# Convolution taps regrouped around the waits of VectorE in a fused encoder layer

## The chip, the cores and the metric

One core of a Trainium2 chip (trn2) runs the whole kernel as one launch. The metric is the device time in microseconds (us), lower being better. Names of engines: PE is TensorE, DVE is VectorE, ACT is ScalarE, POOL is GpSimd, SP is SyncE.

## What is computed

One layer of an encoder for 16 meta tokens, a prompt of 512 frames and a sample of 32 frames with cached keys, values and convolution rows. All in float32, model width 1024, 16 heads of 64, convolution width 31. Cut to what matters:

```python
glu, q, k, v, gates = _in_proj(_rmsnorm(x, g_mix), w_in)      # glu = a * sigmoid(b)
y = depthwise_conv(ctx, w_dw) + b_dw                          # 31 taps, causal, per channel
conv_out = silu(_layernorm(y, g_ln, b_ln)) @ w_pw2
z = q . k * HEAD_DIM ** -0.5                                  # per head, strictly causal mask
log_1m = where(mask, log_sigmoid(-z), 0.0)
tail = cumsum(log_1m, reverse=True) - log_1m
attn_out = where(mask, exp(log_sigmoid(z) + tail), 0.0) @ v
x = x + (sigmoid(g_conv) * conv_out + sigmoid(g_attn) * attn_out) @ w_out
x = x + square(relu(_rmsnorm(x, g_mlp) @ w_up)) @ w_down
y_out = _rmsnorm(x, g_final)
```

Outputs are y for both groups, the new keys and values, and the last 30 GLU rows of each group.

## The kernel before

Activations lie transposed, channels on the 128 partitions and up to 560 tokens along the free axis. Each matrix product is done in three passes of split operands (high by high, high by low, low by high); a weight tile of 1024 x 128 is split by ACT (w_hi, and the negated raw copy in w_lo) and finished by a DMA that adds the raw tile to w_lo.

After loading and normalising x comes the channel loop: eight turns, i = 0 to 7, one for each block of 128 channels, which are two heads and 128 convolution channels. A turn has six projections on PE, each 48 matmuls: q (unit 0), k (unit 1), v (unit 2), a (unit 3), b (unit 4), gate of the attention (unit 5). Turn 0 is written out, and turns 1 to 7 are one hardware loop. Every engine runs its own list in order, as written by hand, and waits on counting semaphores. PE's list in turns 1 to 7 is: units 0 and 1; `cumulate` of the second head of the turn before; unit 2; `values` of the turn before (the product with v, into PSUM bank 3 and a part of bank 1); `scores` of the first head; the transposes of v; units 3 and 4; `cumulate` of the first head; unit 5; `scores` of the second head.

In `scores` of the first head, banks 0 and 2 are done first. Bank 1 still holds the sample's 32 columns that `values` has left there, so PE waits for `mix_s_done` before the masks that open that bank:

```python
                if not early:
                    pe.wait_ge(mix_s_done, i)
                    masks_1()
```

This is the mask L639 that stands behind the matmuls of 144 columns (L635) in the timeline. `mix_s_done` comes from the first instruction of DVE's `gate_mix` (L1372), which reads those columns; L1373 reads bank 3. `gate_mix(prev)` itself waits for `pv_done` (PE's `values`) and `ga_done` (ACT).

`softplus_logs` on ACT turns scores into log(1 + exp(-|z|)) (L1014, L1019, L1024), DVE's `softplus_sum` (L1401) adds max(z, 0), `tile_sums` (L1419 to L1434) folds sums over tiles, ACT rounds (L1032, L1036), and DVE forms the low parts (L1407 and, in `sums_low`, L1438). `cumulate` on PE (L671, L691) needs these, and needs L1438 for its products with `negones`; ACT then takes exponentials (L1048). For the convolution's gate, ACT computes its logarithm (L1002 to L1006) from unit 4, DVE subtracts (L1490), ACT takes the exponential (L1113), and DVE multiplies into `conv_in` (L1492). The attention's gate goes likewise over L1002 to L1006 and DVE's L1377.

The 31 taps of the depthwise convolution are DVE instructions over 574 columns (L1362 for taps 0 and 1, L1365 for the rest), one for each tap and block. Taps of channel block i start at the end of turn i (groups 0 and 1 of the list `CONV`), and the rest is spread over turn i + 1 between the steps that other engines wait for, by `conv_before(n)`, which does group n. Turn 0 has no block before it. The block of turn 7 is finished behind the loop, in one string of 20 taps. L1515 behind the loop is the last step like L1438; a load of weights into the ring's fourth slot on SP waits for it.

Of the kernel before, what the change touches and what calls it, by code (L numbers as in the profile page):

```python
# [24 lines left out]
TAPS = 31  # L25
# [59 lines left out]
def build(nc, x_prompt, x_sample, cache_k, cache_v, cache_conv, meta, g_mix, w_in, w_dw, b_dw,  # L85
# [25 lines left out]
    with ExitStack() as ctx:  # L111
# [180 lines left out]
        def tile(i, t):  # L292
            return X_TILES + LOOP_TILES * i + t
# [27 lines left out]
        def cols2(ap, half):  # L321
            return ap.rearrange("p (h c) -> p h c", c=half)
# [17 lines left out]
        def x_half(t, h):  # L340
            (_, col, n), = X_COLS[t]
            return xT[:, h * KC // 2:(h + 1) * KC // 2, col:col + n]
# [199 lines left out]
        def _(pe):  # L542
# [63 lines left out]
            def scores(i, hh, first=False):  # L606
# [47 lines left out]
                for j in (2, 3):  # L654
                    bank, off, _, q0 = KT[j]
                    mm = score_split(bank, off, j, q0)
                mm.then_inc(z_scored, 1)
# [3 lines that stand above are left out]
                bank, off, _, q0 = KT[1]  # L661
                score_split(bank, off, 1, q0)
                score_last().then_inc(z_scored, 1)
# [642 lines left out]
        def _(dve):  # L1306
# [50 lines left out]
            def conv(i, taps):  # L1357

                for k in taps:
                    src, w, dst = conv_in[:, META + k:META + k + CONV_COLS], cw_cur[:, PAD + k:PAD + k + 1], acc[:, k % 2, :]  # L1360
                    if k < 2:
                        nc.vector.tensor_scalar(dst, src, w, None, ALU.mult).then_inc(tap_done, 1)  # L1362
                    else:
                        dve.wait_ge(tap_done, TAPS * i + k - 1)
                        nc.vector.scalar_tensor_tensor(dst, src, w, dst, ALU.mult, ALU.add).then_inc(tap_done, 1)  # L1365

            def gate_mix(i):

                mixed_cur = mixed[:, bass.ds(i, 1), :].rearrange("p n c -> p (n c)")
                dve.wait_ge(ga_done, i + 1)  # L1370
                dve.wait_ge(pv_done, i + 1)
                nc.vector.tensor_tensor(mixed_cur[:, SEQ:], z[:, 1, S_PV:S_PV + DEC], gate_a[:, SEQ:], ALU.mult).then_inc(mix_s_done, 1)  # L1372
                nc.vector.tensor_tensor(mixed_cur[:, 0:SEQ], pv[:], gate_a[:, 0:SEQ], ALU.mult).then_inc(mix_done, 1)  # L1373

            def attn_gate(i):
                dve.wait_ge(ga_ln, i + 1)
                nc.vector.scalar_tensor_tensor(cols2(gate_a[:], HALFO), psum2(1, HALFO), 0.0, cols2(gate_a[:], HALFO), ALU.min, ALU.subtract).then_inc(ga_log, 1)  # L1377
# [8 lines left out]
                nc.vector.tensor_tensor(sum_y[:], sum_y[:], y_cur, ALU.add).then_inc(sumy_done, 1)  # L1386


            CONV = [range(a, b) for a, b in ((0, 8), (8, 11), (11, 12), (12, 20), (20, 24), (24, 26), (26, TAPS))]

            def turn(i, prev=None):
                first = prev is None
                def conv_before(n):
                    if not first:
                        conv(prev, CONV[n])

                def softplus_sum(head, n, hh):
                    sp = heads2[hh]
                    b, c = BANKS[n], BANK_COLS[BANKS[n]]
                    dve.wait_ge(log_done, 3 * head + n + 1)  # L1400
                    nc.vector.scalar_tensor_tensor(sp[:, b, 0:c], z[:, b, 0:c], 0.0, sp[:, b, 0:c], ALU.max, ALU.add).then_inc(sp_done, 1)  # L1401
# [34 lines left out]
                def sums_low(head):  # L1436
                    dve.wait_ge(sumshi_done, head + 1)
                    nc.vector.tensor_tensor(sums_both[UPPER], sums, sums_both[LOWER].bitcast(F32), ALU.subtract).then_inc(sumslo_done, 1)  # L1438

                def keep_keys(t, src, dst, kept):  # L1440
                    dve.wait_ge(tile_done, tile(i, t) + 1)
                    nc.vector.tensor_copy(cols2(dst[:, 0:TOK], HALF), src[:, :, 0:HALF])
                    nc.vector.tensor_copy(dst[:, TOK:TOK + META], src[:, 0, 0:META]).then_inc(kept, 1)
# [20 lines left out]
                nc.vector.transpose(ckT[:], ck_blk[:]).then_inc(ck_turned, 1)  # L1464
                conv_before(3)
                keep_keys(T_V, z[:, 0:2] if first else dense[:, 0], vT, v_kept)
                if not first:
                    gate_mix(prev)
                conv_before(4)
                for n in range(3):  # L1470
                    softplus_sum(2 * i, n, 0)
                    if n == 0:
                        conv_before(5)
                tile_sums(2 * i, 0)
                for n in range(3):
                    softplus_low(2 * i, n, 0)
                sums_low(2 * i)
                conv_before(6)
                if not first:
                    conv_end(prev)  # L1480

# [13 lines left out]
                dve.wait_ge(cur_done, i + 1)  # L1495
                conv(i, CONV[0])

# [4 lines left out]
                attn_gate(i)  # L1502
                conv(i, CONV[1])
                for n in range(3):
                    softplus_sum(2 * i + 1, n, 1)
                tile_sums(2 * i + 1, 1)
                for n in range(3):
                    softplus_low(2 * i + 1, n, 1)

            turn(0)  # L1510
            with dve.Fori(0, KC - 1) as before:
                turn(before + 1, before)

            dve.wait_ge(sumshi_done, 2 * KC)
            nc.vector.tensor_tensor(sums_both[UPPER], sums, sums_both[LOWER].bitcast(F32), ALU.subtract).then_inc(sumslo_done, 1)  # L1515
            for taps in CONV[2:]:
                conv(KC - 1, taps)
# [184 lines left out]
```

## Time and profile before

| | us |
|---|---|
| median of 3 runs | 954.9 |
| lowest and highest | 954.67, 956.01 |
| the profiled execution | 954.9 |
| its span, first to last instruction | 953.1 |
| PE busy | 941.6 |
| DVE busy | 540.0 |
| ACT busy | 523.5 |
| POOL busy | 257.1 |

The granted TensorE clock is 0.998 of full speed over the span. An engine's busy time is summed over the whole span; the channel loop ends near 414 us, and what comes behind it leaves DVE and ACT mostly idle. In the timeline an instruction's row gives its start and its length; where instructions follow each other in a pipeline, the next one starts before the one ahead has ended, and the distance of two starts is the cost of the one ahead. Square brackets at a row's end give the idle time of the engine ahead of it and who ended it.

### The profile page before, as it was taken

What the parts mean: (1) busy time and instruction counts of PE and PEld (TensorE: products, weight loads), DVE (VectorE), ACT (ScalarE), POOL (GpSimd) and SP (SyncE); (2) the same over time, 40 slices, a digit from 0 to 9 for tenths busy, and PEclk for the clock granted to TensorE, in tenths of its full rate; (3) what the DMA queues carried; (4) which work ended last, traced back from release to release, by engine and by line L of the source; (5) the groups of instructions that cost most, each with busy time, mean ns of one, the idle gap of its engine ahead of it and who ended that gap; (6) DMA issues with size and microseconds to landing.
All of it is one profiled execution on the core that took longest, in us unless ns stands there. A gap on an engine that the chain in (4) does not pass through costs nothing.

```text
span 953.1 us, 19728 instructions
## 1 busy us (share of the span) xinstructions
PE 941.6 (99%) x7473; PEld 923.4 (97%) x7473; DVE 540.0 (57%) x931; ACT 523.5 (55%) x810; POOL 257.1 (27%) x188
## 2 busy tenths in 40 slices
PE   8999999999999999999999999999999999999997
PEld 8999999999999999989999999999999999999997
DVE  6579999999999999996653322222111122221133
ACT  6787878878787878786733343333111133331153
POOL 5311110101010101012243444445334244453340
PEclk9999999999999999999999999999999999999999
DMA  6777676766767575668132223333223133343102
GB/s 180 161 169 146 152 144 157 131 170 122 178 118 182 111 189 104 148 155 199 46 110 80 82 83 104 86 92 116 89 88 88 48 89 88 90 125 91 45 23 95
DMA packets 189520, 111.37 MB, mean 117 GB/s; under 512 B 35437, under 2 KB 181277, under 8 KB 189482
## 3 DMA queue, kind: packets, MB, share of 16 engines
q1 hardware_dynamic: 176666, 80.28, 30.5%
q0 software_dynamic: 7632, 27.79, 16.1%
q10 hardware_dynamic: 5184, 2.78, 1.0%
q8 instruction: 26, 0.43, 0.2%
q14 instruction: 12, 0.10, 0.0%
HBM read 75.97 MB, written 7.06 MB: 87 GB/s over the span
## 4 chain that ended last, share of the span: by engine, by line
PE 92%; DVE 3%; issue 1%; DMA 1%; POOL 1%; ACT 1%; DVEq 0%; POOLq 0%
PE dense L551 78%; PE z L671 3%; PE dense L846 3%; PE z L635 2%; PE z L705 2%; POOL w_lo L516 1%; DMA w_lo<-w_raw 1%; PE z L551 1%; DVE acc L1365 1%; PE z L565 1%; PE z L639 0%; PE dense L715 0%; PE z L838 0%; DMA w_raw<-in_w_in_dram 0%; PE z L629 0%
## 5 line engine op out<-in xcount | busy, mean ns | idle before, releaser
L534 POOL TENSOR_TENSOR w_lo<-w_raw,w_hi 128x1024 fp32r<-128x1024 f32 x80 | 192.2, 2405 | 295.1 <-ACT w_hi L939 295.1
L551 PE MATMUL dense<-r_hi,w_hi 128*128 128x272 f32 (+1 forms) x1264 | 263.6, 291 | 2.8 <-DMA w_lo<-w_raw 2.2
L551 PE MATMUL dense<-r_lo,w_hi 128*128 128x272 f32 (+1 forms) x1264 | 262.6, 289 | 0.0
L551 PE MATMUL dense<-r_hi,w_lo 128*128 128x272 f32 (+1 forms) x1264 | 262.2, 289 | 0.0
L939 ACT ACTIVATE w_hi<-w_raw 128x1024 fp32r<-128x1024 f32 x134 | 140.7, 1052 | 115.0 <-PE dense L551 102.7
L551 PEld LDWEIGHTS dense<-r_hi,w_hi 128*128 128x128 f32 x1264 | 198.1, 188 | 3.2 <-DMA w_lo<-w_raw 2.3
L551 PEld LDWEIGHTS dense<-r_lo,w_hi 128*128 128x128 f32 x1264 | 198.9, 188 | 0.7 <-DVE r_lo L1346 0.6
L551 PEld LDWEIGHTS dense<-r_hi,w_lo 128*128 128x128 f32 x1264 | 199.1, 188 | 0.0
L1365 DVE SCALAR_TENSOR_TENSOR acc<-conv_in,cw_cur,acc 128x574 f32<-128x574 f32 x232 | 172.8, 810 | 0.5
L511 POOL DMA_DIRECT2D w_lo<-w_raw x53 | 45.1, 851 | 363.2 <-ACT w_lo L941 363.2
L551 PE MATMUL dense<-s_hi,w_hi 128*128 128x272 f32 x640 | 132.2, 288 | 0.0
L551 PE MATMUL dense<-s_hi,w_lo 128*128 128x272 f32 x640 | 131.6, 288 | 0.0
L551 PE MATMUL dense<-s_lo,w_hi 128*128 128x272 f32 x640 | 131.4, 287 | 0.0
L1561 DVE TENSOR_TENSOR xT<-dense,xT 128x544 f32 (+1 forms) x36 | 26.1, 725 | 159.2 <-PE dense L551 159.2
L551 PEld LDWEIGHTS dense<-s_lo,w_hi 128*128 128x128 f32 x640 | 100.0, 188 | 0.0
L551 PEld LDWEIGHTS dense<-s_hi,w_hi 128*128 128x128 f32 x640 | 99.7, 188 | 0.1
L551 PEld LDWEIGHTS dense<-s_hi,w_lo 128*128 128x128 f32 x640 | 99.7, 189 | 0.0
L1210 ACT ACTIVATE n<-n 128x544 f32<-128x544 f32 x32 | 21.1, 659 | 119.0 <-DVE n L1589 119.0
L1589 DVE SCALAR_TENSOR_TENSOR n<-dense,rstd 128x544 f32<-128x544 f32 x32 | 23.2, 725 | 95.5 <-PE dense L551 90.5
L941 ACT ACTIVATE w_lo<-w_raw 128x1024 fp32r<-128x1024 f32 x53 | 55.6, 1048 | 0.0
L551 PE MATMUL dense<-u_hi,w_hi 128*128 128x272 f32 x192 | 39.8, 288 | 0.0
L551 PE MATMUL dense<-u_hi,w_lo 128*128 128x272 f32 x192 | 39.5, 288 | 0.0
(258 smaller groups left out, 1288.9 us busy)
## 6 DMA issues: line engine op xcount, KB each, us to landing
w_raw<-in_w_in_dram SPq DMA_DIRECT2D x54, 512.0 KB, 5.8
w_lo<-w_raw POOLq DMA_DIRECT2D x53, 512.0 KB, 5.0
w_raw<-in_w_up_dram SPq DMA_DIRECT2D x32, 512.0 KB, 4.0
w_raw<-in_w_down_dram SPq DMA_DIRECT2D x32, 512.0 KB, 3.5
w_raw<-in_w_pw_dram SPq DMA_DIRECT2D x8, 512.0 KB, 3.5
w_raw<-in_w_out_dram SPq DMA_DIRECT2D x8, 512.0 KB, 3.6
x_tok<-in_x_prompt_dram SPq DMA_DIRECT2D x4, 512.0 KB, 5.7
out_dram<-k_blk SPq DMA_DIRECT2D x32, 64.0 KB, 3.6
```

Of the source, the lines that this page charges most:

```text
L511: pool.dma_start(w_lo[:, s].bitcast(F32), w_raw[:, s], accum_op=ALU.add).then_inc(lo_done[s], 16)
L534: pool.tensor_tensor(w_lo[:, n], w_raw[:, n], w_hi[:, n].bitcast(F32), ALU.subtract).then_inc(lo_post, 1)
L551: mm = nc.tensor.matmul(out[:, h, 0:half], w[:, wslot, k, :], m[:, k, c0 + h * half:c0 + (h + 1) * half], start=(k == 0 and n == 0), stop= ...
L635: mm = nc.tensor.matmul(z[:, bank, off:off + SEQ - q0], k_both[:, hh, j * P:(j + 1) * P], qp[:, hh, q0:SEQ], start=False, stop=False, skip ...
L671: mm = nc.tensor.matmul(z[:, dst[0], dst[1]:dst[1] + n], m[:], part_[src], start=False, stop=False, skip_group_check=True)
L846: mm = nc.tensor.matmul(part_out(n, p), w[:, n, k, :], m[:, k, cols], start=(k == 0 and j == 0), stop=(k == KC - 1 and j == 2))
L939: done = nc.scalar.activation(w_hi[:, s], w_raw[:, s], ACT.Copy)
L941: done = nc.scalar.activation(w_lo[:, s], w_raw[:, s], ACT.Copy, scale=-1.0)
L1210: nc.scalar.activation(n32[:, n % 2, 0:OUTTOK], n32[:, n % 2, 0:OUTTOK], ACT.Square).then_inc(u32_done, 1)
L1365: nc.vector.scalar_tensor_tensor(dst, src, w, dst, ALU.mult, ALU.add).then_inc(tap_done, 1)
L1561: nc.vector.tensor_tensor(cols2(x_cur, HALFO), psum2(slot, HALFO), cols2(x_cur, HALFO), ALU.add).then_inc(emptied[slot], 1)
L1589: nc.vector.scalar_tensor_tensor(cols2(n32[:, n % 2, 0:OUTTOK], HALFO), psum2(n % 2, HALFO), 0.0, cols2(rstd[:, 0:OUTTOK], HALFO), ALU.max ...
```

## The change

The list of tap groups gets other bounds and one more group, and `conv_before` is called once more in a turn. Groups 0 to 2 stay as they are.

```diff
-            CONV = [range(a, b) for a, b in ((0, 8), (8, 11), (11, 12), (12, 20), (20, 24), (24, 26), (26, TAPS))]
+            CONV = [range(a, b) for a, b in ((0, 8), (8, 11), (11, 12), (12, 21), (21, 24), (24, 28), (28, 29), (29, TAPS))]
...
                 conv_before(3)
                 keep_keys(T_V, z[:, 0:2] if first else dense[:, 0], vT, v_kept)
+                conv_before(4)
                 if not first:
                     gate_mix(prev)
-                conv_before(4)
+                conv_before(5)
                 for n in range(3):
                     softplus_sum(2 * i, n, 0)
                     if n == 0:
-                        conv_before(5)
+                        conv_before(6)
...
-                conv_before(6)
+                conv_before(7)
                 if not first:
                     conv_end(prev)
```

Taps per place in a turn, before and after: ahead of the copy of v 8 and 9; between the copy and `gate_mix` 0 and 3; between `gate_mix` and the first softplus sum 4 and 4; between the first and second softplus sum 2 and 1; behind `sums_low` 5 and 2. The lists of PE, ACT, POOL and SP are the same. Behind the changed call DVE's lines have numbers higher by one.

DVE in turns 1 to 7, from the last tap ahead of the copy of v (L1442, L1443) over `gate_mix` (L1372, L1373) to the next taps, before:

```order
118 L1365 SCALAR_TENSOR_TENSOR acc<-conv_in,cw_cur,acc 128x574 [waits tap_done]
119 L1441 ISA
120 L1442 COPY vT<-dense 128x560 [waits tile_done]
121 L1443 COPY vT<-dense 128x16
122 L1372 ISA [waits pv_done,ga_done]
123 L1372 TENSOR_TENSOR mixed<-z,gate_a 128x32
124 L1373 ISA
125 L1373 TENSOR_TENSOR mixed<-z,gate_a 128x512
```

The same place after:

```order
122 L1442 COPY vT<-dense 128x560 [waits tile_done]
123 L1443 COPY vT<-dense 128x16
124 L1364 REGISTER_ALU
125 L1365 SCALAR_TENSOR_TENSOR acc<-conv_in,cw_cur,acc 128x574 [waits tap_done]
126 L1364 REGISTER_ALU
127 L1365 SCALAR_TENSOR_TENSOR acc<-conv_in,cw_cur,acc 128x574 [waits tap_done]
128 L1364 REGISTER_ALU
129 L1365 SCALAR_TENSOR_TENSOR acc<-conv_in,cw_cur,acc 128x574 [waits tap_done]
130 L1372 ISA [waits pv_done,ga_done]
131 L1372 TENSOR_TENSOR mixed<-z,gate_a 128x32
```

Three taps now stand between the copy of v and `gate_mix`, and one more ahead of the copy.

DVE a little further on, from the first softplus sum of the first head to the second, before:

```order
135 L1401 SCALAR_TENSOR_TENSOR sp<-z,sp 128x512 [waits log_done]
136 L1364 REGISTER_ALU
137 L1365 SCALAR_TENSOR_TENSOR acc<-conv_in,cw_cur,acc 128x574 [waits tap_done]
138 L1364 REGISTER_ALU
139 L1365 SCALAR_TENSOR_TENSOR acc<-conv_in,cw_cur,acc 128x574 [waits tap_done]
140 L1400 REGISTER_ALU
141 L1401 SCALAR_TENSOR_TENSOR sp<-z,sp 128x480 [waits log_done]
```

The same place after:

```order
143 L1401 SCALAR_TENSOR_TENSOR sp<-z,sp 128x512 [waits log_done]
144 L1364 REGISTER_ALU
145 L1365 SCALAR_TENSOR_TENSOR acc<-conv_in,cw_cur,acc 128x574 [waits tap_done]
146 L1400 REGISTER_ALU
147 L1401 SCALAR_TENSOR_TENSOR sp<-z,sp 128x480 [waits log_done]
```

One tap has moved out from between the two sums, and three have moved out from behind L1438.

PE's list around its wait for `gate_mix`, the same before and after:

```order
360 L635 MATMUL z<-q_low,k_both 128x272
361 L635 MATMUL z<-q_twice,k_both 128x144
362 L635 MATMUL z<-q_low,k_both 128x144
363 L639 MATMUL z<-neg_diag,ident_b 128x128 [waits mix_s_done]
364 L639 MATMUL z<-neg_last,ident_b 128x48
365 L635 MATMUL z<-q_twice,k_both 128x400
366 L635 MATMUL z<-q_low,k_both 128x400
367 L621 MATMUL z<-q_end,k_end 128x48
368 L715 MATMUL dense<-ident,vT 128x128 [waits v_kept]
```

Nothing moves here; the wait at L639 is for the instruction that now stands behind four more taps.

## Rows read from the trace of the kernel before

**Rows 1.** The page: span, chain by engine, and the taps' group (line, count | busy, mean ns)

```profile
span 953.1 us, 19728 instructions
...
PE 92%; DVE 3%; issue 1%; DMA 1%; POOL 1%; ACT 1%; DVEq 0%; POOLq 0%
...
L1365 DVE SCALAR_TENSOR_TENSOR acc<-conv_in,cw_cur,acc 128x574 f32<-128x574 f32 x232 | 172.8, 810 | 0.5
```

**Rows 2.** The chain that ended last, its longest pieces: start us, us, what

```profile
136.87 0.57 PE dense L715 x5
...
331.36 0.57 PE dense L715 x5
...
428.28 6.28 PE dense L551 x48
...
435.47 12.02 PE dense L551 x96
```

**Rows 3.** Busy time by stretch: length, PE, PEld, DVE, ACT, POOL, clock, DMA share, GB/s

```profile
330.00:379.00 49.00, 49.00 (x389) 47.09 (x389) 47.02 (x88) 38.82 (x66) 5.39 (x7) 1.00 0.68 148
```

**Rows 4.** PE's timeline, turns 6 and 7: start us, us, engine line op out<-in

```profile
345.35 0.27 PE L671 MATMUL z<-sp_lo,own_own 128*128 128x48 f32 x1
345.46 0.33 PE L671 MATMUL z<-w_hi,negones 128*128 128x176 f32 x1
...
367.76 0.27 PE L671 MATMUL z<-sp_lo,own_own 128*128 128x48 f32 x1
367.94 0.35 PE L671 MATMUL z<-w_hi,negones 128*128 128x176 f32 x1
...
379.12 0.23 PE L639 MATMUL z<-neg_diag,ident_b 128*128 128x128 bf16 x1
```

**Rows 5.** DVE's timeline in turn 7 and behind the loop

```profile
366.85 1.03 DVE L1438 TENSOR_TENSOR w_hi<-w_raw,w_hi 64x848 fp32r<-64x848 f32 x1
...
378.14 0.18 DVE L1372 TENSOR_TENSOR mixed<-z,gate_a 128x32 f32 x1
...
378.83 2.99 DVE L1365 SCALAR_TENSOR_TENSOR acc<-conv_in,cw_cur,acc 128x574 f32<-128x574 f32 x4
381.95 0.69 DVE L1401 SCALAR_TENSOR_TENSOR sp<-z,sp 128x512 f32<-128x512 f32 x1
...
414.86 14.64 DVE L1365 SCALAR_TENSOR_TENSOR acc<-conv_in,cw_cur,acc 128x574 f32<-128x574 f32 x20
```

**Rows 6.** The chain that ended last, every piece of 376 to 434

```profile
381.39 0.53 ACT sp L1024
...
414.86 3.93 DMA w_raw<-in_w_in_dram
```

**Rows 7.** Timelines of ACT and DVE in turn 6, around the convolution's gate

```profile
346.21 1.04 ACT L939 ACTIVATE w_hi<-w_raw 128x1024 fp32r<-128x1024 f32 x1
347.16 1.04 ACT L941 ACTIVATE w_lo<-w_raw 128x1024 fp32r<-128x1024 f32 x1
348.88 0.67 ACT L1113 ACTIVATE gate_b<-gate_b 128x560 f32<-128x560 f32 x1 [0.68 <-DVE gate_b L1490]
...
349.59 0.71 DVE L1492 TENSOR_TENSOR conv_in<-a_sb,gate_b 128x528 f32<-128x528 f32 x1 [0.74 <-ACT gate_b L1113]
```

**Rows 8.** Timelines of ACT and DVE in turn 6, attention's gate and second head

```profile
353.74 0.66 ACT L1006 ACTIVATE gate_a<-gate_a 128x544 f32<-128x544 f32 x1
...
357.66 1.07 ACT L1024 ACTIVATE ez<-ez 128x480 f32<-128x480 f32 x2
...
355.82 0.69 DVE L1377 SCALAR_TENSOR_TENSOR gate_a<-dense,gate_a 128x544 f32<-128x544 f32 x1
...
358.60 1.79 DVE L1401 SCALAR_TENSOR_TENSOR ez<-z,ez 128x512 f32<-128x512 f32 x3
```

**Rows 9.** Timelines of PE and ACT behind the loop, where the next weight is awaited

```profile
428.28 0.52 PE L551 MATMUL dense<-r_hi,w_hi 128*128 128x272 f32 x2 [2.22 <-DMA w_lo<-w_raw]
...
417.27 1.50 ACT L1048 ACTIVATE ez<-z 128x512 f32<-128x512 f32 x3 [3.75 <-PE z L671]
```

## The prediction

> **What bounds the kernel now.** I read the page's shares first, then the chain that ended last, then the timelines of PE, DVE and ACT over turns 6 and 7 of the channel loop. The profiled execution took 954.9 us, 1.8 us more than its span of 953.1, and the median of the runs is 954.9 as well, so sums go on 954.9.
>
> PE carries 92% of the chain [rows 1]. So the time changes by what PE loses or stops losing. In the loop one turn lasts 48.6 us on PE: the transposes of v start at 136.87 in turn 2 and at 331.36 in turn 6 [rows 2], and (331.36 - 136.87) / 4 = 48.62. In 330 to 379 PE is busy all 49 us, but DVE is nearly full too, with 47.02 [rows 3], so it can't be moved freely against PE: each hand-over in either direction has a margin of its own, and those margins are what the change uses.
>
> Four hand-overs matter.
> - DVE to PE, twice. PE's last sums of a head (L671 with negones) start at 367.94, and the DVE step that they need (L1438) ends at 366.85 + 1.03 = 367.88. The matmul ahead started at 367.76, 0.18 before, where the same pair in the other head stands 345.46 - 345.35 = 0.11 apart: PE waits 0.07 us here in each turn [rows 4]. And the mask L639 of the first head's scores starts at 379.12. It waits for mix_s_done, which DVE gives with L1372, at 378.14 + 0.18 = 378.32. Adding the 0.06 that PE needed behind L1438 (367.94 against 367.88), the mask could have started at 378.38: a margin of 0.74 [rows 4, 5].
> - PE to DVE, over ACT. The first softplus sum of a turn (L1401) starts at 381.95, and ACT's logarithm for it ends in the chain at 381.39 + 0.53 = 381.92, so DVE is held there, by about 0.1 us (its taps end at 378.83 + 2.99 = 381.82) [rows 5, 6]. Later in the turn DVE waits for ACT's exponential of gate_b (L1113), which itself stood 0.68 idle until DVE's L1490. ACT's work ahead of it (L1002 to L941) is fed by PE's projection b (unit 4): were PE later by more than 0.68, this exponential would be late, and DVE's L1492 with it [rows 7].
>
> **The change, part by part.** No instruction is added or removed. Seven turns of DVE (1 to 7) get another order, and the 20 taps behind the loop are one unbroken string before and after. One tap costs 0.73 us: the string of 20 takes 14.64, less its last tap's 0.81, over 19 is 0.728 [rows 1, 5]. Four taps are 2.91.
>
> 1. One tap more ahead of the copy of v, then three between the copy and gate_mix. Nothing hides them: DVE goes from the taps over the copy to L1372 (378.14) and on to the next taps (378.83) with no idle time shown [rows 5]. The copy itself comes 0.73 later, but its reader on PE, L715, is queued behind the mask: free. L1372 starts 2.91 later, at 381.05, and PE could go on at 381.05 + 0.18 + 0.06 = 381.29 instead of 379.12. **PE stands 2.17 us** in turn 1, the first time. All that is queued on PE behind that mask stands with it: three matmuls of the scores, the transposes, two projections.
>
> 2. One tap less between the first two softplus sums, three less behind L1438. The four taps come back here. DVE is four taps late at its first softplus sum (2.8 us, since the 0.1 of waiting there goes), three at the second and up to L1438 (2.1), and level again at the end of the convolution. PE's cumulate needs this L1438, which comes 2.1 later, but PE itself is then 2.17 later. Free.
>
> 3. What PE's delay does to DVE. From turn 1 on PE is behind DVE by 2.17 more than before. If DVE never had to wait for PE, it would keep its old pace and PE would pay 2.17 once. But the exponential L1113 has a margin of 0.68 by the idle time shown; an ACT instruction that waits for nothing starts 0.09 before the one ahead has ended (346.21 + 1.04 = 347.25 against 347.16), so it may be 0.77 [rows 7]. DVE is pushed by 2.17 - 0.68 = 1.49, or 2.17 - 0.77 = 1.40. I take 1.45. DVE's own string to the next L1372 holds nothing that could absorb it, so the next mask is late by that again, and PE stands 1.45 us in each of the turns 2 to 7. The other PE-to-DVE margins are wider: 355.82 - (353.74 + 0.66) = 1.42 at gate_a's logarithm, about 359.78 - 358.73 = 1.05 at the third softplus sum of the second head (358.60 + 1.79 for three, less a third, against 357.66 + 1.07) [rows 8]. They push less than L1113 does and add nothing.
> Sum at turn 7's mask: 2.17 + 6 x 1.45 = 10.87.
>
> 4. The end of the loop. The DMA of w_lo for the next weight lands 2.22 us late for PE (428.28) [rows 9], behind two ends that are level today: the load of w_raw, released by DVE's L1515, lands at 414.86 + 3.93 = 418.79, and ACT's exponentials end at 417.27 + 1.50 = 418.77 [rows 6, 9]. The exponentials follow PE (ACT stood 3.75 us for it), hence come 10.87 later; by the same 0.09 overlap ACT was ready at 418.68, so 0.11 of that is saved. The DVE side comes only 7 x 1.45 = 10.15 later and is no longer last. The 2.22 stays. **10.76 us reach the end**, since PE then runs on without a gap and DVE and ACT have idle time there.
>
> 5. What is won: the 0.07 us wait at PE's L671 of the second head goes, as PE comes 2.17 later there and DVE only 1.45. The new round of waits (mask, projection b, L1113, L1372, mask) doesn't pass that matmul, so its length, and the sum, are as above.
>
> 954.9 + 10.76 = 965.66; I give 965.6.
>
> **A rule weighed.** After the 2.22 us wait PE does 48 matmuls of 272 columns in 6.28 us, 0.131 each, and then 96 in 12.02, 0.125 each [rows 2]: it doesn't win time back. The Trainium skill (TensorE: Matmul & The Clock Gate, Back-to-back issue gap) gives an isolated matmul the spacing N / 2.4 + 2.5 ns, by my working from that page an estimate of 116 ns at 272 columns, where this trace has 125. By the page a turn's 288 dense matmuls would have about 2.6 us in reserve, more than 1.45, and the sum would fall to the rival of one stall. The trace disagrees with that, so it stays a rival.
>
> **Rivals.**
> - *Another margin decides.* If ACT's exponential isn't the one that pushes DVE, the softplus sums are: 2.17 - 1.05 = 1.12 per turn, 2.17 + 6 x 1.12 - 0.11 = 8.78, **963.7**. With gate_a's 1.42 it is 0.75 per turn, 6.56, 961.5. For: the three hand-overs lie close together. Against: ACT's idle of 0.68 is a plain row.
> - *One stall only.* PE makes its delay good between the masks, or DVE has a reserve that I didn't see, so that after turn 1 nothing is pushed: 2.17 - 0.11, **957.0**. PE would need 1.45 us on 288 dense matmuls, 5 ns each. Against: its pace after the 2.22 us.
> - *Nothing is absorbed.* DVE is tied to PE without any margin, and each of the seven stalls is whole: 7 x 2.17 - 0.11 = 15.1, **970.0**. For: the first softplus sum has such a tie today. Against: four taps ahead of it loosen it by 2.8.
> - *Not slower.* The loop is bound by the round that goes from PE's scores over ACT to the first softplus sum, over DVE to L1438, and to PE's L671; four taps leave that round. This is where the 0.07 us wait is won, seven times, 0.5 us: **954.4**. It decides if the mask L639 can bear four taps, that is from a margin of 2.91 on. The rows show 0.74 in turn 7, and nothing in the order lets DVE come earlier. For: both ends of that round are tight. Against: PE's wait for mix_s_done has no other cover than those 0.74.
>
> **How the numbers follow.** Forecast 965.6: 0.62 (964.8 to 966.6, by the margin of 0.68 or 0.77, a tenth more or less per restart of PE, and the landing of the last DMA). Another margin: 0.18. One stall: 0.08. Not slower: 0.07. Nothing absorbed: 0.05. The forecast and the wider margins make the 8 in 10: 961.5 to 966.6, to which I add a little above for latencies that I set at 0.06 per hand-over and that repeat seven times: 961.2 to 968.0. A difference under 0.2% (1.9 us) is about what a measurement of this kernel can't tell from no change: 953.0 to 956.8. The case not slower lies within it, 957.0 on its edge, half to each side; faster by more has only what is left. Faster 0.01, same 0.10, slower 0.89.
>
> **What would show it.** In the profile after: before L639 (the one behind the 144 columns) PE stands some 2.2 us in turn 1 and about 1.45 in turns 2 to 7, released by DVE's mixed; the loop's turns are 50.0 to 50.1 us long; ACT shows no idle time before L1113, and DVE's idle before the gate product (L1492, L1493 there) grows from 0.74 to some 1.8 us; the first softplus sum no longer follows ACT's logarithm at once; dense matmuls keep 0.125 to 0.128 us and the granted clock 1.00. I am wrong if turns stay at 48.6 after turn 1 (one stall), if they are 49.4 to 49.8 with ACT still idle before L1113 (another margin), or if PE never waits at the mask.

## The result and the profile after

| | before | after |
|---|---|---|
| median, us | 954.8 (4 runs, 954.24 to 956.01) | 965.1 (4 runs, 964.13 to 965.98) |
| profiled execution, its span | 954.9, 953.1 | 963.9, 962.1 |

The changed kernel is slower by 1.06% (ratio 1.0106, 95% interval 1.0094 to 1.0119). The forecast was 965.6, in a range of 961.2 to 968.0.

The page of the changed kernel, its span, PE's busy time and the chain by engine. PE's busy time is what it was to 0.1% (942.3 against 941.6), so the span has grown by waits. PE's share of the chain fell from 92% to 83% [rows 1]; the second traces of the two kernels have 86% and 83%, so only the direction says something here.

```profile
span 962.1 us, 19728 instructions
...
PE 942.3 (98%) x7473; PEld 923.1 (96%) x7473; DVE 540.0 (56%) x931; ACT 523.4 (54%) x810; POOL 257.2 (27%) x188
...
PE 83%; issue 7%; DVE 5%; ACT 2%; DMA 1%; SPq 1%; DVEq 0%; POOL 0%; ACTq 0%; POOLq 0%
```

What PE waited for (us in total, times, longest us), two lines of the list:

```profile
PE z L639 <- DVE mixed L1372: 9.8, 7, 2.0
...
PE dense L551 <- DMA w_lo<-w_raw: 0.6, 1, 0.6
```

The first line is new: seven waits at the mask, for gate_mix. The second corresponds to the 2.22 us in [rows 9].

PE's timeline around the mask, in turns 1, 2 and 7 (compare [rows 4]):

```profile
87.28 0.27 PE L635 MATMUL z<-q_low,k_both 128*128 128x144 f32 x1
89.55 0.23 PE L639 MATMUL z<-neg_diag,ident_b 128*128 128x128 bf16 x1 [2.00 <-DVE mixed L1372]
...
139.54 0.23 PE L639 MATMUL z<-neg_diag,ident_b 128*128 128x128 bf16 x1 [1.29 <-DVE mixed L1372]
...
388.14 0.27 PE L635 MATMUL z<-q_low,k_both 128*128 128x144 f32 x1
389.73 0.23 PE L639 MATMUL z<-neg_diag,ident_b 128*128 128x128 bf16 x1 [1.32 <-DVE mixed L1372]
```

The figure in brackets starts at the modelled end of the matmul ahead, 0.27 behind its start. Where nothing holds the mask it starts 0.11 or 0.12 behind that matmul's start (0.11 in turn 1 of the kernel before; 137.23 and 137.35 in the two-tap kernel below). So PE lost 89.55 - 87.28 - 0.11 = 2.16 us in turn 1, and 1.59 - 0.11 = 1.48 in turn 7.

DVE in turn 1, around gate_mix, and in turns 1 and 2 further on (compare [rows 5, 7]):

```profile
86.40 0.73 DVE L1442 COPY vT<-dense 128x560 f32<-128x560 f32 x1
87.05 0.17 DVE L1443 COPY vT<-dense 128x16 f32<-128x16 f32 x1
87.13 2.27 DVE L1365 SCALAR_TENSOR_TENSOR acc<-conv_in,cw_cur,acc 128x574 f32<-128x574 f32 x3
89.31 0.18 DVE L1372 TENSOR_TENSOR mixed<-z,gate_a 128x32 f32 x1
...
105.39 0.74 DVE L1491 SCALAR_TENSOR_TENSOR gate_b<-dense,gate_b 128x560 f32<-128x560 f32 x1 [0.51 <-ACT gate_b L1006]
107.84 0.71 DVE L1493 TENSOR_TENSOR conv_in<-a_sb,gate_b 128x528 f32<-128x528 f32 x1 [1.71 <-ACT gate_b L1113]
...
139.30 0.18 DVE L1372 TENSOR_TENSOR mixed<-z,gate_a 128x32 f32 x1
```

The mask on PE starts 89.55 - (89.31 + 0.18) = 0.06 us behind the end of gate_mix's first instruction. From one gate_mix to the next are 139.30 - 89.31 = 49.99 us; the later turns have 49.99 to 50.06, where they had 48.62.

ACT in the same turn, up to the exponential of gate_b (compare [rows 7]):

```profile
105.26 1.05 ACT L939 ACTIVATE w_hi<-w_raw 128x1024 fp32r<-128x1024 f32 x1
106.21 1.04 ACT L941 ACTIVATE w_lo<-w_raw 128x1024 fp32r<-128x1024 f32 x1
107.16 0.65 ACT L1113 ACTIVATE gate_b<-gate_b 128x560 f32<-128x560 f32 x1
```

L1113 has no idle time ahead of it any more. It runs as soon as ACT has done the weight, and DVE is the one that waits, 1.71 us where it waited 0.74.

DVE has one more new wait, which the prediction doesn't list: 0.50 to 0.57 us in each turn at L1491, where it subtracts and needs ACT's logarithm (L1006). In turn 3 of the kernel before, the same subtraction started at 202.25 and the logarithm had ended at 199.77 + 0.67 = 200.44, so this hand-over had a margin of 1.81 us. It is passed too, but L1113's margin is the smaller one and decides.

Behind the loop (compare [rows 6, 9]), from the timelines of DVE, ACT and PE, and the DMA from the chain:

```profile
423.61 1.04 DVE L1516 TENSOR_TENSOR w_hi<-w_raw,w_hi 64x848 fp32r<-64x848 f32 x1
...
427.87 1.50 ACT L1048 ACTIVATE ez<-z 128x512 f32<-128x512 f32 x3 [4.55 <-PE z L671]
429.25 1.07 ACT L939 ACTIVATE w_hi<-w_raw 128x1024 fp32r<-128x1024 f32 x1
...
431.56 5.65 DMA w_lo<-w_raw
...
437.25 0.52 PE L551 MATMUL dense<-r_hi,w_hi 128*128 128x272 f32 x2 [0.58 <-DMA w_lo<-w_raw]
```

ACT goes from its exponentials to L939 without a gap, so PE's lag decides here, as forecast. But the DMA took 5.65 us where it had taken 7.12, and PE's wait shrank from 2.22 to 0.58, by 1.64: 1.47 from the DMA, the rest from ACT, which had no wait for the load any more. The lag at the loop's last mask was 389.73 - 379.12 = 10.61 us; 10.61 less 1.64 is the 9.0 us between the two spans.

### The profile page after: what moved, and what is told of

The parts are those of the page before. It is cut to its first block, busy times and chain, and to the rows that moved or that the text cites. A ratio compares the mean times of both kernels' runs of the same rounds, so it can differ in the third digit from the quotient of the medians.

```text
span 962.1 us, 19728 instructions
## 1 busy us (share of the span) xinstructions
PE 942.3 (98%) x7473; PEld 923.1 (96%) x7473; DVE 540.0 (56%) x931; ACT 523.4 (54%) x810; POOL 257.2 (27%) x188
## 4 chain that ended last, share of the span: by engine, by line
PE 83%; issue 7%; DVE 5%; ACT 2%; DMA 1%; SPq 1%; DVEq 0%; POOL 0%; ACTq 0%; POOLq 0%
PE dense L551 74%; DVE acc L1365 3%; PE dense L846 3%; PE z L671 2%; PE z L635 1%; DMA w_lo<-w_raw 1%; DMA w_raw<-in_w_in_dram 1%; PE z L565 1%; ACT k_both L1085 0%; PE dense L715 0%; PE z L838 0%; SPq L374 0%; PE z L639 0%; PE dense L578 0%; DVE ckT L1464 0%
## 5 line engine op out<-in xcount | busy, mean ns | idle before, releaser
L939 ACT ACTIVATE w_hi<-w_raw 128x1024 fp32r<-128x1024 f32 x134 | 140.7, 1052 | 114.7 <-PE dense L551 102.7
```

Source lines behind the costliest of these rows:

```text
L939: done = nc.scalar.activation(w_hi[:, s], w_raw[:, s], ACT.Copy)
```

## The experiments

Each kernel is the changed one with one edit, but for the one with five taps and PE kept busy, which has two, and the last two, which are the kernel before and the changed one again. A ratio is against runs of the kernel before on the same chip; medians of different kernels come from different chips, and the kernel before had 954.6 to 956.0 there.

### The mask waits for gate_mix, and for nothing else

**Gate_mix ahead of all four moved taps.**

```diff
-            ... (12, 21), (21, 24), (24, 28) ...
+            ... (12, 20), (20, 22), (22, 28) ...
...
-                conv_before(4)
                 if not first:
                     gate_mix(prev)
+                conv_before(4)
                 conv_before(5)
```

> The changed kernel with its four taps still ahead of the first softplus sum, but all of them behind gate_mix, and with 8 taps ahead of the copy of v as before: DVE comes to the softplus sum as late as in the changed kernel, to gate_mix as early as before. Theory (the mask on PE waits for gate_mix): no stall at L639, turns of 48.6 us or a little less, 954.3 us, 0.5 less than before by the wait at PE's L671 (0.07 us a turn). Rival (the late softplus sum costs the time, by the chain over ACT to cumulate): about 965, as changed, with turns of 50.0. Second rival (no cost, no gain): 954.8.

Measured: 953.96, ratio 0.9993 (0.9984 to 1.0002). Turns are 48.50 to 48.55 us long, and PE waits at no mask that stands behind gate_mix. DVE reaches the first softplus sum as late as in the changed kernel, and it costs nothing. So the late softplus sum is not the cause; the place of gate_mix is. The gain in the loop is too small for the timing, but the traces show it: turns went from 48.62 to 48.53, since PE's wait of 0.07 at L671 is gone.

**Gate_mix cut in two.** Only its first instruction, for the sample's 32 columns, is put back ahead of the three taps. The two functions in the cut below hold one instruction of gate_mix each.

```diff
+                if not first:
+                    gate_mix_sample(prev)
                 conv_before(4)
                 if not first:
-                    gate_mix(prev)
+                    gate_mix_prompt(prev)
```

> The changed kernel with gate_mix cut in two: its first instruction (L1372, the sample's 32 columns, gives mix_s_done) goes ahead of the three taps, its second (L1373, bank 3, gives mix_done) stays behind them. Only L1372's place differs from the changed kernel. Theory: the mask waits for L1372 alone; it then comes one tap later than before (0.73 us against a margin of 0.74), no stall over 0.1 us, 954.4 to 955. Rival (L1373 or bank 3 holds PE, or DVE's order in general): 965, with a wait at PE's values or at the mask.

Measured: 953.21, ratio 0.9984 (0.9975 to 0.9993). DVE's timeline in turn 2, where L1379 is the small instruction and L1383 the large one:

```profile
134.97 0.16 DVE L1453 COPY vT<-dense 128x16 f32<-128x16 f32 x1
135.05 0.18 DVE L1379 TENSOR_TENSOR mixed<-z,gate_a 128x32 f32 x1
135.15 2.26 DVE L1365 SCALAR_TENSOR_TENSOR acc<-conv_in,cw_cur,acc 128x574 f32<-128x574 f32 x3
137.33 0.68 DVE L1383 TENSOR_TENSOR mixed<-z,gate_a 128x512 f32 x1
```

The instruction that gives mix_done still stands behind the taps, and no one misses it. All that cost 10 us is an instruction of 0.18 us standing behind three taps. The time came out some 1 us below what was expected, for a reason shown further down.

### How the cost grows with the taps

The same kernel with gate_mix one, two, three and five taps late instead of four; the total of taps ahead of the first softplus sum is the same in all. For one tap, gate_mix is called ahead of `conv_before(4)`; for the others the groups are:

```diff
-            ... (12, 21), (21, 24), (24, 28) ...
+            ... (12, 21), (21, 22), (22, 28) ...     two taps late
+            ... (12, 21), (21, 23), (23, 28) ...     three
+            ... (12, 21), (21, 25), (25, 28) ...     five
```

> The changed kernel with gate_mix directly behind the copy of v, one tap late in place of four (9 taps ahead of the copy, none between, seven behind). Theory of two margins: 0.728 us against a margin of 0.74 at the mask, no stall, 954.3 to 954.9. Rival (in proportion to taps): 957.4.

> The changed kernel with gate_mix two taps late in place of four: one more ahead of the copy of v, one between the copy and gate_mix, six behind gate_mix. Theory of two margins: the mask is late by 2 x 0.728 - 0.74 = 0.72 us in turn 1, which is less than the 0.79 that DVE can bear, so nothing is pushed and turns 2 to 7 lose nothing more: 0.7 us in all, 955.5, turns of 48.6. Rival (each turn pays its stall, no margin on DVE's side): 7 x 0.72 = 5.0, 959.8, turns of 49.35. Rival (cost in proportion to taps): half of 10.3, 960.

> The changed kernel with gate_mix three taps late in place of four (one ahead of the copy, two between, five behind gate_mix). Theory of two margins: stall of 3 x 0.728 - 0.74 = 1.44 us in turn 1, push of 1.44 - 0.79 = 0.65 in each turn, turns of 49.3: 1.44 + 6 x 0.65 = 5.3, 960.1. Rival (each stall paid in full): 7 x 1.44 = 10.1, 964.9. Rival (in proportion): 962.5.

> The changed kernel with gate_mix five taps late in place of four (one ahead of the copy, four between, three behind gate_mix). Theory of two margins: stall of 5 x 0.728 - 0.74 = 2.90 us in turn 1, push of 2.11 in each turn, turns of 50.7: 2.90 + 6 x 2.11 = 15.6, 970.4. From four taps to five that is 7 x 0.728 = 5.1 more. Rival (each stall paid in full): 20.3, 975.1. Rival (in proportion): 967.7.

| taps late | PE held in turn 1, forecast / measured | the six turns from turn 1's gate_mix to turn 7's, forecast / measured | median, us | ratio, interval |
|---|---|---|---|---|
| 1 | none / none | no longer / 48.4 to 48.5 | 953.3 | 0.9979 (0.9969 to 0.9990) |
| 2 | 0.72 / idle 0.55 | 48.6 / 48.58 to 48.60 | 954.15 | 0.9989 (0.9980 to 0.9998) |
| 3 | 1.44 / idle 1.27 | 49.3 / 49.25 to 49.33 | 958.8 | 1.0040 (1.0026 to 1.0054) |
| 4 | 2.17 / idle 2.00 | 50.07 / 49.99 to 50.06 | 965.1 | 1.0106 (1.0094 to 1.0119) |
| 5 | 2.90 / idle 2.74 | 50.7 / 50.77 to 53.6 | 977.9 | 1.0226 (1.0205 to 1.0246) |

(The turn is the distance of two L1372; "idle" is the bracket in the trace, which counts 0.16 less than PE lost, see above.) PE's timeline with two taps, in turns 1 and 2:

```profile
88.77 0.23 PE L639 MATMUL z<-neg_diag,ident_b 128*128 128x128 bf16 x1 [0.55 <-DVE mixed L1372]
...
137.23 0.27 PE L635 MATMUL z<-q_low,k_both 128*128 128x144 f32 x1
137.35 0.23 PE L639 MATMUL z<-neg_diag,ident_b 128*128 128x128 bf16 x1
```

It stands once and never again: 0.72 us of lag are less than DVE can bear, so PE's phase moves once and the delay isn't paid again. They are only just less: DVE's wait at the gate product has grown from 0.74 to 0.93 us in every turn, so it is already held there, but not so long that the next mask comes late. With three taps the waits at the mask go on, 0.57 us in each later turn:

```profile
137.56 0.23 PE L639 MATMUL z<-neg_diag,ident_b 128*128 128x128 bf16 x1 [0.57 <-DVE mixed L1372]
...
186.82 0.23 PE L639 MATMUL z<-neg_diag,ident_b 128*128 128x128 bf16 x1 [0.56 <-DVE mixed L1372]
```

So there are two thresholds, and the rivals "each stall paid in full" (959.8 with two taps, 964.9 with three) and "in proportion" are out. The first margin, 0.74 us, is PE's at the mask. The second, some 0.7 to 0.8, is DVE's: with four taps 2.16 less the 1.41 us by which the turns grew, 0.75. What passes both is paid in every turn.

The times with one, two and three taps came out 1.0 to 1.6 us below what was expected. The stalls are as forecast; the difference is the wait behind the loop, which the forecasts had left at 2.22 us (see below).

### Where PE's delay reaches DVE

**ACT's exponential ahead of the weight.**

```diff
-                high_ahead(7)
                 act.wait_ge(gb_log, i + 1)
                 nc.scalar.activation(gate_b[:], gate_b[:], ACT.Exp).then_inc(gb_done, 1)
+                high_ahead(7)
```

> The changed kernel with ACT's exponential of gate_b (L1113) ahead of the split of the next weight (L939, L941), not behind it. Theory (PE's delay reaches DVE over L1113, since ACT does the weight first): DVE is then pushed only by the next margin, the softplus sums of the second head (1.05 us): 2.16 - 1.05 = 1.1 a turn instead of 1.37, turns of 49.75 us instead of 49.99, 2.16 + 6 x 1.1 = 8.8 us in all, 963.5. Rival (another hand-over pushes DVE already): turns stay 49.99, 965.1. Rival (nothing pushes DVE once L1113 is out of the way, one stall only): turns of 48.6, 957.

Measured: 962.31, ratio 1.0080 (1.0065 to 1.0096), turns of 49.90 to 49.94. DVE's waits for ACT in turn 3:

```profile
204.57 0.74 DVE L1491 SCALAR_TENSOR_TENSOR gate_b<-dense,gate_b 128x560 f32<-128x560 f32 x1 [0.57 <-ACT gate_b L1006]
206.05 0.71 DVE L1493 TENSOR_TENSOR conv_in<-a_sb,gate_b 128x528 f32<-128x528 f32 x1 [0.74 <-ACT gate_b L1112]
...
212.65 0.72 DVE L1377 SCALAR_TENSOR_TENSOR gate_a<-dense,gate_a 128x544 f32<-128x544 f32 x1 [0.29 <-ACT gate_a L1006]
...
216.52 1.19 DVE L1401 SCALAR_TENSOR_TENSOR ez<-z,ez 128x480 f32<-128x480 f32 x2 [0.27 <-ACT ez L1024]
```

The wait at L1491 is the one that the changed kernel has too. The wait at the gate product is back to its 0.74, and two new ones have come where there had been none: at the attention's gate and at the second softplus sum of the second head. So L1113 was the hand-over that decided how far DVE is pushed, and the others together push nearly as far. The turn shrank by only 0.1 us, not by the 0.25 expected: the margin at the softplus sums is about 2.16 - (49.93 - 48.62) = 0.85, not 1.05 (2.16 is the lag that four taps give; in turn 1 PE was held 1.58 here, since turn 0 put DVE 0.74 us earlier). I had read it at the third sum; the wait shows at the second. The rival that nothing else would push is out. The two spans differ by 1.5 us: 0.74 in turn 0, where the exponential comes earlier too (the first L1372 starts at 88.57 where it was at 89.31), 0.6 in the six turns, and 0.26 in the wait behind the loop (0.32 for 0.58). The 2.8 us between the medians, from two chips, are more than that; no trace shows the rest.

### The fifth tap and the clock

With five taps the forecast of 970.4 failed, and the kernel (977.9) was slower even than the rival with each stall paid in full (975.1). Two turns of three were 52.3 to 53.6 us long, the others 50.77. Busy time by stretch of that kernel (the columns are those of [rows 3]), behind the waits of turns 1, 2, 3, 4 and 5:

```profile
90.00:94.00 4.00, 3.14 (x15) 3.14 (x16) 3.63 (x7) 1.64 (x4) 0.00 (x0) 0.50 0.93 175
...
146.00:150.00 4.00, 4.00 (x27) 4.00 (x26) 3.69 (x8) 3.27 (x8) 0.00 (x0) 0.77 1.00 237
...
198.00:206.00 8.00, 8.00 (x65) 8.00 (x64) 7.76 (x18) 5.90 (x13) 0.00 (x0) 1.00 1.11 263
247.00:252.00 5.00, 4.64 (x21) 4.64 (x22) 4.63 (x9) 3.15 (x7) 0.00 (x0) 0.50 0.99 194
...
300.00:306.00 6.00, 5.02 (x29) 5.02 (x29) 5.97 (x11) 3.77 (x9) 0.00 (x0) 0.72 1.03 206
```

The granted clock is 0.50 behind the first and the fourth wait, the lower of its two levels (1.2 GHz), a mean of 0.77 and 0.72 behind the second and the fifth, where it is down for a part of the stretch, and 1.00 behind the third, whose turn is one of the 50.77. In all it fell at five of the seven waits; the third and the sixth, with the two turns of 50.77, are the others. The waits of turns 1, 3 and 4:

```profile
90.86 0.29 PE L639 MATMUL z<-neg_diag,ident_b 128*128 128x128 bf16 x1 [2.74 <-DVE mixed L1372]
...
196.59 0.23 PE L639 MATMUL z<-neg_diag,ident_b 128*128 128x128 bf16 x1 [2.01 <-DVE mixed L1372]
...
247.36 0.29 PE L639 MATMUL z<-neg_diag,ident_b 128*128 128x128 bf16 x1 [2.03 <-DVE mixed L1372]
```

The third and the fourth wait have the same length, and the clock fell at one of them only; the mask itself takes 0.29 us where the clock had fallen by then and 0.23 in turn 3. What sets the third wait apart is not shown. The Trainium skill (TensorE: Matmul & The Clock Gate, Part 1: The HAM clock gate) says that a clock gate halves the array's clock when the array has been idle, and that its look at the engine runs free of the kernel. The trace agrees with the first: 0.50 behind PE's waits, and 1.00 in the next kernel, where PE is idle for only 0.90 us of the first. That equal waits of 2.0 us end differently fits the second, but doesn't show it.

**PE kept busy at the mask**, in the kernel with five taps.

```diff
                 if not early:
+                    for _ in range(8):
+                        nc.tensor.matmul(dense[:, 1, 0, 0:P], ones[:], ones[:], start=True, stop=True)
                     pe.wait_ge(mix_s_done, i)
```

> The kernel with five taps ahead of gate_mix, in which PE does eight matmuls of ones (128 columns, float32) into a free part of PSUM while it would stand at the mask; their result is never read. In the run of five taps the granted clock read 0.50 for some microseconds behind some of the waits, and two turns of three were 52.3 to 53.6 us long where the third was 50.77. Theory (the extra over 970.4 is the clock, which falls where PE stands 2.0 to 2.7 us at the mask among short matmuls): with PE busy there the clock stays at 1.00, all turns are 50.77, about 970.5. Rival (the extra is a wait or a transfer that comes late at this lag): 978 still, turns uneven.

Measured: 969.48, ratio 1.0146 (1.0129 to 1.0163). The same stretch, and the wait:

```profile
90.00:94.00 4.00, 3.35 (x28) 3.35 (x29) 4.00 (x8) 2.46 (x6) 0.00 (x0) 1.00 0.86 162
```

```profile
90.65 0.23 PE L639 MATMUL z<-neg_diag,ident_b 128*128 128x128 bf16 x1 [0.90 <-DVE mixed L1374]
```

The masks now stand 50.71 to 50.79 us apart in all turns, and 8.4 us are gone from the median (10.1 from the span), although PE does more work. The two-margin sum gave 970.4 without the clock; it holds, and the clock was the rest.

**The changed kernel with PE kept busy**, five such matmuls in place of eight.

> The changed kernel, in which PE does five matmuls of ones (128 columns, float32, some 0.24 us each) into a free part of PSUM while it would stand at the mask; their result is never read. They fit into its stalls of 1.3 us and leave its order of work alone. The changed kernel's runs lay in two groups, 963.9 to 965.0 at a mean clock of 0.998 and 965.4 to 966.2 at 0.996 or 0.997. Theory (the upper group has its clock fallen behind a stall in some turn): with PE busy all runs lie in the lower group, 964.3 in the median. Rival (the spread comes from elsewhere, as it does in the kernel before): 965.0 with the same spread. Either way turns of 50.0 us: the stall is not PE's own work.

Measured: 964.72, ratio 1.0106 (1.0089 to 1.0122), runs from 963.5 to 965.4, the highest at a mean clock of 0.999. The spread of 1.8 us stayed, so it isn't the clock; the theory fell and the rival stands. PE's idle time at the mask went from 2.00 to 0.86 us in turn 1 and from 1.3 to 0.15 in turns 2 and 3, and not a microsecond was won. A stall that is filled is still a stall.

### The wait behind the loop

> The kernel before, unchanged, for a second trace. Its PE stood 2.22 us behind the loop for a DMA of w_lo that took 7.12 us; every other kernel here stood 0.32 to 1.05 us. If that DMA's time is set by when DVE's L1515 lets the load of w_raw go, against ACT's chain (4.0 us between them before, 4.6 in most others), the wait is 2.2 again. If it varies from run to run, it is anywhere between 0.3 and 2.3. Turns of 48.61 either way.

> The changed kernel, unchanged, for a second trace. Turns of 49.99 to 50.05 again; the wait behind the loop 0.6 us if it is set by the order of releases, 0.3 to 2.3 if it varies from run to run.

Measured: 955.52 and 964.95, one execution of each; spans 953.7 and 963.1. The wait behind the loop in the two traces of each, from PE's timelines (the first traces are in [rows 9] and above):

```profile
428.11 0.52 PE L551 MATMUL dense<-r_hi,w_hi 128*128 128x272 f32 x2 [1.59 <-DMA w_lo<-w_raw]
```

```profile
438.15 0.52 PE L551 MATMUL dense<-r_hi,w_hi 128*128 128x272 f32 x2 [0.72 <-DMA w_lo<-w_raw]
```

Both effects are there. The same kernel gives 2.22 and 1.59, so the landing varies by half a microsecond. And every kernel in which DVE reaches its last sum earlier against ACT's chain has less: 0.32 to 0.95 in the ten traces of nine kernels. From the release of the weight's load (the end of DVE's last sum) to the start of the w_lo DMA were 421.11 - 414.86 = 6.25 us before, 6.3 in its second trace and in the first experiment, and 6.9 to 7.0 in those ten. The first experiment's wait, 1.05, lies between the two groups. The DMA's own time fell from 7.12 and 6.44 to 5.65 and 5.79. That the two transfers get less in each other's way is the likely reason; it wasn't tried apart.

This also accounts for the kernels that beat the one before. With one tap late, PE's turns are 48.54 us (mask to mask) in place of 48.61, 0.5 us over seven, and the wait behind the loop is 0.62 in place of 1.59 to 2.22: 1.5 to 2.1 us, against 1.7 measured.

## Why the prediction was right

1. **The stall at the mask.** Predicted 2.17 us in turn 1 from four taps of 0.728 against a margin of 0.74; measured 2.16 (2.18 in the second trace). The 0.06 us from DVE's end to PE's start held as well.
2. **The push on DVE by L1113.** Predicted 1.45 us a turn, turns of 50.0 to 50.1; measured 49.99 to 50.06. The named signs came: no idle ahead of L1113, DVE's wait at the gate product 1.71 where 1.8 was said. The exchange of ACT's two steps showed that this hand-over was the one, and that the next stood 0.1 us behind it, nearer than the forecast had it (0.33: 1.45 against 1.12). The prediction left out the hand-over at L1491; with a margin of 1.81 us it decided nothing.
3. **The lag at turn 7's mask.** Predicted 10.87, measured 10.61. The turns grew by 1.41 us, not 1.45: 2.16 + 6 x 1.41 = 10.6. PE was held 1.48 at each of these masks, and what is more than 1.41 is the wait of 0.07 at L671 that went; step 5 of the prediction, that this gain is already in the sum, was right.
4. **The end of the loop, the step that was off.** "The 2.22 stays" failed: 0.58 and 0.72 stayed. The order of releases that the prediction itself worked out (DVE's side 0.7 us earlier than PE's) is the likely reason that the DMA got shorter; it wasn't tried apart. That term should have been a gain of some 1 us with its own spread. It brings the traces' difference to 9.0 and 9.4 us where 10.7 was said. Between the medians it is 10.3, and what makes up the last microsecond no trace shows. So the stalls and the turns were predicted, but that the median came within 0.5 us of the forecast is partly luck.
5. **The rivals.** "Another margin decides" had the right mechanism for the exchanged kernel, with a push of 1.31 us a turn in place of its 1.12, and not for this one. "One stall only" came true at two taps, where the lag stays within DVE's margin; its form with PE winning time back came nowhere. "Nothing is absorbed" is out by the kernels with two and three taps. "Not slower" was right about its round and price: once the mask is spared, the four taps ahead of the softplus sum win the 0.07 us a turn.
6. **The rule weighed.** No trace shows PE winning back time after a stall. The estimate of 116 ns from the Trainium skill (TensorE: Matmul & The Clock Gate, Back-to-back issue gap) for 272 columns is nowhere in these runs; in the changed kernel 96 dense matmuls behind the loop took 12.02 us, 125 ns each, as before. The section gives that spacing for an isolated matmul and says that in a stream with weight loads both set the pace, so the prediction's reserve of 2.6 us was not one that it promises.

## What to carry to other kernels

When two engines are both nearly full, look up the margin of every hand-over between them, in both directions, before moving work. A step that comes late by less than the first margin costs nothing; between the margins it costs one shift of phase; beyond both it costs the excess in every turn, here 3.8, 10.3 and, with the clock held up, 13.5 us for three, four and five taps. An instruction of a fifth of a microsecond that another engine waits for belongs ahead of filler work, even if the rest of its step doesn't.

## What the runs showed of the hardware

With five taps the granted clock fell at five of PE's seven waits of 2.01 to 2.74 us, to 0.50 for the next 4 us behind those of 2.74 and 2.03. It didn't fall behind two of 2.01, nor behind the 2.22 us of the kernel before, nor behind the 2.00 or the six of 1.3 of the changed one. It made one tap more cost 12.8 us in place of 5. Eight useless matmuls in that wait brought 8.4 us back. The sum for five taps had counted on a clock of 1.00, as the kernel before shows it behind a single wait of 2.22 us; that is no safe ground for a wait of 2 us that repeats in every turn.
